# Eight start offsets, modulo 256 bytes, for the ring of split hidden features in a two-layer hybrid transformer kernel

## The chip, the cores and the metric

The kernel runs on one core of a Trainium2 chip. The metric is the device time of one execution in microseconds (us). Times of the kernel before: 1723.94 us as the median of three runs (1721.37, 1723.94 and 1724.77). TensorE (PE in the rows) multiplies, VectorE (DVE) and ScalarE (ACT) do the elementwise work, GpSimd (POOL) a little of it, and DMAs issued by SyncE (SP) bring the weights in.

## What is computed

One sequence of 256 tokens with 16 meta tokens ahead (272 in all) and 1024 features goes through two layers. Each layer is: feed-forward, mixer (a retention group and a differential attention group on one input projection), feed-forward. Then a third block follows with an attention over context and a mixture of 32 experts. The part that the change touches is the feed-forward:

```python
def swiglu(x, w_gate, w_up, w_down):
    return (jax.nn.silu(x @ w_gate) * (x @ w_up)) @ w_down

for l in range(DEPTH):                                   # DEPTH = 2, D_FF = 2816 = 22 * 128
    h = h + 0.5 * swiglu(rmsnorm(h, ffn1_norm[l]), ffn1_w_gate[l], ffn1_w_up[l], ffn1_w_down[l])
    ...                                                  # mixer
    h = h + 0.5 * swiglu(rmsnorm(h, ffn2_norm[l]), ffn2_w_gate[l], ffn2_w_up[l], ffn2_w_down[l])
```

So there are four feed-forwards, f = 0 to 3. "The middle" is silu(gate) * up, 2816 features of 272 tokens. In the last one (f = 3) the 16 meta tokens are dropped, and 256 tokens are left.

## The kernel before

**Tiles.** Features lie on the 128 partitions, tokens along the free dimension. `h` has 8 chunks of 128 features (C = 8), the middle has 22 (F = 22). Weights stream from memory through `ring`, 8 KB per partition and slot (L623 to L710 issue the loads).

**Three products for one.** Every fp32 operand a is split into a_hi, a rounded copy (ScalarE), and a_lo = a - a_hi (VectorE), both of type fp32r. The weights are split in the same way into four buffers `w_split` (L1536 on ScalarE, L2011 on VectorE). One product is then three matmuls, in `product` (L769 to L771): w_hi with x_hi, w_hi with x_lo, w_lo with x_hi. The stationary operand is 128 by 128 from `w_split`, the moving operand has 272 columns (256 where the meta tokens are left out).

**A feed-forward.** In `ffn` (L808 on) a gate and up stage of 22 steps multiplies the eight chunks `x_hi[c]`, `x_lo[c]`; then the down stage goes over the 22 chunks i of the middle. In it `part(i, o)` is one product for output chunk o, for 8 values of o, so each chunk i of the middle is the moving operand of 24 matmuls in a row, and a down stage has 22 * 8 * 3 = 528 matmuls.

**The middle's ring.** The split chunks of the middle are `hid_hi` and `hid_lo`, eight places each (`HID_SPLITS`), chunk i in place i % 8. L1602 (ScalarE, `hidden_hi`) writes the high part and L2122 (VectorE, `hidden_lo`) the low part. Place c of `hid_hi` begins at word `hid_at + c * STEP` of the tensor `arena`, where `STEP` is 320 words (1280 bytes, five times 256), and a place is 272 words long, which leaves a gap of 48 words. The helper `spaced` (L296) cuts them, and also the eight places of `x_hi` and `x_lo`.

**Start addresses.** They follow from the allocation: `ring` begins at byte 16512 of each partition and `arena` at byte 114816, both 128 modulo 256. Every weight tile in `w_split` begins at 128 modulo 256. The places of `x_hi` and `x_lo` all begin at 64 modulo 256, and those of `x_hi_late`, `x_lo_late` (the second layer's mixer) at 0; a window of 256 tokens in these begins 64 bytes later, at 64. The places of `hid_hi` and `hid_lo` all begin at 32; in f = 3, `t_at` is 8 words, so what is read begins at 64. The chunks of `y_hi`, `y_lo` are 1088 bytes apart in the first layer, so these begin at 0, 64, 128 and 192 in turn; in the second layer they are 1024 bytes apart and all begin at 64. The experts' weights that are moving operands (L1423) begin at 128 in `ring` and at 12 in `con`.

**What else hangs on the ring's end.** `hid_end` (L294) is where it stops. `mod_product` begins there (eight chunks in which ScalarE, L1615, and VectorE, L2110 and L2112, form the sums of a modulation vector, beside the gate and up stages), and `x2n` ends half there (`at_x2n = hid_end - C * SEQ`, L369): it is the normalised input of the third block, the moving operand of L1090, L1096 and L1102 and the stationary one of L1108, between about 1084 and 1213 us.

**Order.** Each engine runs its list in program order. The experts' weights (L689 to L710) are loaded from the moment that `y2_ready` has its last count, given by VectorE at L2591.

Of the kernel before, what the change touches and what calls it, by code (L numbers as in the profile page):

```python
# [15 lines left out]
META, SEQ = 16, 256  # L16
T = META + SEQ
DEPTH = 2
FF = 2816
F = FF // P  # L20
# [16 lines left out]
HALF = SLOT // 2  # L37
QUARTER = HALF // 2
HID_SPLITS = 8
STEP, LEAD, HID_LEAD = 320, 48, 8  # L40
GAP = STEP - T
ARENA = 20768
IN2_SLOTS = 11
# [189 lines left out]
def build(nc, stream_ffn, stream_in, stream_out, stream_mod, stream_in2, stream_out2, stream_expert,  # L233
# [4 lines left out]
    with ExitStack() as ctx:  # L238
# [10 lines left out]
        arena_at = nc.sbuf_base - 4 * ARENA  # L249
# [6 lines left out]
        def cut(tensor, at, *shape):  # L256

            n = int(np.prod(shape))
            piece = tensor[:, at:at + n]
            if len(shape) == 1:  # L260
                return piece
            names = "abcd"[:len(shape)]
            sizes = dict(zip(names[1:], shape[1:]))
            return piece.rearrange(f"p ({' '.join(names)}) -> p {' '.join(names)}", **sizes)
# [21 lines left out]
        def parts(name, byte, *shape):  # L286

            n = int(np.prod(shape))
            return cut(nc.alloc_sbuf_tensor_at(name, [P, n], f32r, offset=byte), 0, *shape)


        rest = C * T + LEAD + 2 * C * STEP - GAP
        hid_at = rest + F * T + HID_LEAD
        hid_end = hid_at + 2 * HID_SPLITS * STEP - GAP  # L294
        h = cut(arena, 0, C, T)
        def spaced(name, at, n):  # L296

            return [parts(f"{name}{c}", arena_at + 4 * (at + c * STEP), T) for c in range(n)]

        x_hi, x_lo = spaced("x_hi", C * T + LEAD, C), spaced("x_lo", C * T + LEAD + C * STEP, C)  # L300
        x_hi_late, x_lo_late = spaced("x_hi_late", C * T + LEAD - META, C), spaced("x_lo_late", C * T + LEAD - META + C * STEP, C)
# [6 lines left out]
        hid = cut(arena, rest, F, T)  # L308
        gate_act = cut(con, CON["axial_cos"][0], 4, T)
        warm = cut(arena, rest, 513)  # L310
        hid_hi, hid_lo = spaced("hid_hi", hid_at, HID_SPLITS), spaced("hid_lo", hid_at + HID_SPLITS * STEP, HID_SPLITS)
        assert hid_end <= ARENA and 4 * T <= CON["causal"][0] - CON["axial_cos"][0]
        ffn_sq = hid[:, F - C:]

# [256 lines left out]
        def window(f):  # L571

            return META if f == 2 * DEPTH - 1 else 0
# [177 lines left out]
        def _(pe):  # L751
# [9 lines left out]
            def norm_sum(n):  # L761

                pe.wait_ge(consts_loaded, 16)
                pe.wait_ge(sq_summed, n + 1)
                pe.matmul(ps[:, 7, 0:T], ones, (mix_sq if n % 3 == 1 else ffn_sq)[:, 0], start=True, stop=True).then_inc(sumsq_ready, 1)

            def product(to, w, k, hi, lo, first, last_):

                pe.matmul(to, w[:, 0, k], hi, start=first, stop=False)  # L769
                pe.matmul(to, w[:, 0, k], lo, start=False, stop=False)  # L770
                return pe.matmul(to, w[:, 1, k], hi, start=False, stop=last_)  # L771

            def split_half(n):

                pe.wait_ge(split_ready, n + 2)
                return w_split[n % SPLITS]

            def first_of_all(n0):

                for k in range(2):  # L780
                    w = w_split[0] if k == 0 else split_half(n0 + k)
                    for c in range(C):
                        if k == 0:
                            pe.wait_ge(x_split_ready, c + 1)
                            pe.wait_ge(split_ready, c // 4 + 1)
                        last = product(ps[:, k, 0:T], w, c, x_hi[c], x_lo[c], c == 0, c == C - 1)
                    last.then_inc(split_used, 1)

            def first_two(n, n0, banks, t=0):

                both = [split_half(n0), split_half(n0 + 1)]
                x_hi, x_lo = stream_of(n)
                for c in range(C):
                    pe.wait_ge(x_split_ready, n * C + c + 1)
                    for k in range(2):
                        last = product(ps[:, banks[k], 0:T - t], both[k], c, x_hi[c][:, 0:T - t], x_lo[c][:, 0:T - t], c == 0, c == C - 1)
                        if c == C - 1:
                            last.then_inc(split_used, 1)

            def features(n, bank, t=0):  # L800

                w = split_half(n)
                for c in range(C):
                    last = product(ps[:, bank, 0:T - t], w, c, x_hi[c][:, 0:T - t], x_lo[c][:, 0:T - t], c == 0, c == C - 1)
                last.then_inc(split_used, 1)

            def ffn(f, n):

                n0 = HALF_AT["ffn", f, 0]
                t = window(f)  # L810
                t_at = META // 2 if t else 0
                if f == 0:
                    first_of_all(n0)
                else:
                    first_two(n, n0, (0, 1), t)
                for j in range(1, F):
                    if j == 2 and f > 0:
                        norm_sum(n)
                    if j == 3:
                        pe.wait_ge(std_ready, n + 1)  # L820
                    if j >= 4:
                        pe.wait_ge(gate_up_used, f * F + j - 3)
                    if f == 2 * DEPTH - 1 and j == CTX_AT:
                        pe.wait_ge(ctx_sq_ready, 1)
                        pe.matmul(ps[:, 2 * (j % 4) + 1, 0:SEQ], ones, ctx_acc, start=True, stop=True).then_inc(ctx_summed, 1)
                    if j in PORTIONS[f]:
                        mod_portion(PORTIONS[f][j], 2 * (j % 4) + 1)
                    for k in range(2):
                        if f == 2 * DEPTH - 1 and j == CTX_AT and k == 1:
                            pe.wait_ge(ctx_std_ready, 1)  # L830
                        if f == 0 and j == 2 and k == 1:
                            norm_sum(n)
                        features(n0 + 2 * j + k, 2 * (j % 4) + k, t)
                down = n0 + 2 * F

                def part(i, o):
                    return product(ps[:, o, 0:T - t], w_split[(down + i) % SPLITS], o, hid_hi[i % HID_SPLITS][:, t_at:t_at + T - t],
                                   hid_lo[i % HID_SPLITS][:, t_at:t_at + T - t], i == 0, i == F - 1)

                for i in range(F - 2):  # L840
                    split_half(down + i)
                    pe.wait_ge(hid_split_ready, f * F + i + 1)
                    for o in (4, 5, 6, 7, 0, 1, 2, 3) if i == 0 else range(C):
                        if i == 0 and o % 2 == 0:
                            pe.wait_ge(gate_up_used, f * F + F - 3 + (o - 4) % C // 2)
                        last = part(i, o)
                    last.then_inc(split_used, 1)
                for i in (F - 2, F - 1):
                    split_half(down + i)
                    pe.wait_ge(hid_split_ready, f * F + i + 1)  # L850
                for o in range(C):
                    last = part(F - 2, o)
                    if o == C - 1:
                        last.then_inc(split_used, 1)
                    part(F - 1, o).then_inc(y_ready if o < C - 1 else split_used, 1)

            def mod_portion(p, bank, col=T):

                batch = int(p >= MOD_FIRST[1])
                n = p - MOD_FIRST[batch]  # L860
                pe.wait_ge(mod_summed, 2 * p + 2)
                if n == 0:
                    pe.wait_ge(mod_ready, batch + 1)
                for i in range(2):
                    for j in range(2):
                        own, at = 2 * n + j, 64 * i + 32 * j
                        last = pe.matmul(ps[at:at + 32, bank, col:col + P], unit_row[:, 32 - own:64 - own], mod_sums[:, p % MOD_BUFFERS, j, i * P:i * P + P],
                                         start=True, stop=True)
                last.then_inc(mod_used, 1)
# [211 lines left out]
            for l in range(DEPTH):  # L1081
                ffn(2 * l, 3 * l)
                mixer(l, 3 * l + 1)
                ffn(2 * l + 1, 3 * l + 2)
# [132 lines left out]
            for i in range(2):  # L1217
                for step in range(6):
                    for hh in range(2):
                        rows = slice(64 * hh, 64 * hh + 64)  # L1220
                        cols = slice((2 * i + hh) * 64, (2 * i + hh) * 64 + 64)
                        to, at = ps[rows, 6 + hh], i * SEQ
                        if step < 2:
                            pe.matmul(to[:, at:at + SEQ], state[rows, 2 * step + i], qx[rows, 2 * step + i], start=step == 0, stop=False)
                        elif step < 4:
                            c = step - 2
# [12 lines left out]
            for i in range(2):  # L1239
                for t in range(2):  # L1240
                    for hh in range(2):
                        head = 2 * i + hh
                        at = (2 * i + t) * P
# [56 lines left out]
            for i in range(2):  # L1300
                for j in range(4):
                    at = 8 * i + 2 * j
# [218 lines left out]
        def _(act):  # L1521
# [43 lines left out]
            def ffn(f, n):  # L1565
# [27 lines left out]
                        act.dma_start(con[:, part], tables[:, part]).then_inc(tables_loaded, 16)  # L1593

                t = window(f)
                t_at = META // 2 if t else 0

                def hidden_hi(i):
                    act.wait_ge(hid_ready, f * F + i + 1)
# [34 lines left out]
                for i in range(F - 2):  # L1634
# [8 lines left out]
                    if f == 2 * DEPTH - 1 and 0 <= i - 9 < C:  # L1643
                        c = i - 9
# [353 lines left out]
        def _(dve):  # L1998
# [74 lines left out]
            def ffn(f, n):  # L2073
# [25 lines left out]
                deviation(n)  # L2099

                t = window(f)
                t_at = META // 2 if t else 0

                def mod_add(u):

# [933 lines left out]
```

## Time and profile before

| | |
|---|---|
| median of three runs | 1723.94 us (1721.37 to 1724.77) |
| the profiled execution | 1728.39 us, of which the span of its instructions is 1726.6 us |
| granted TensorE clock, mean | 0.998 of full speed |
| TensorE matmul busy | 98% of the span, 12315 matmuls |
| VectorE busy | 57% |
| ScalarE busy | 46% |
| DMA mean rate | 247 GB/s |

The span is the time from the first to the last instruction. A matmul's row gives its start and how long it lasted; as matmuls are pipelined, these durations overlap, and what one costs is read from the distance between the starts of neighbours. Where a stretch holds nothing but such matmuls, its length over their number is that distance.

### The profile page before, as it was taken

The numbers are of one execution on the slowest core, as the hardware profiler recorded it, in microseconds if no ns is written. First come the engines' busy times: TensorE is split into PE (matmuls) and PEld (weight loads), VectorE is DVE, ScalarE is ACT, GpSimd is POOL, SyncE is SP. The second block draws the span as 40 slices with busy tenths as digits, with TensorE's granted clock in tenths as the row PEclk, the third lists the DMA queues.
The fourth block names the chain that finished last, engine by engine and source line by source line (L and its number), as shares of the span: only waits on it lengthen the run. The fifth ranks groups of instructions, "written<-read, shape, count | busy, mean of one in ns | idle before, by whom it ended". The sixth has DMA issues, their size and how long they took to land.

```text
span 1726.6 us, 30190 instructions
## 1 busy us (share of the span) xinstructions
PE 1698.7 (98%) x12315; PEld 1392.5 (81%) x12316; DVE 978.0 (57%) x1689; ACT 797.0 (46%) x1432; POOL 168.6 (10%) x173
## 2 busy tenths in 40 slices
PE   9999999999999999999999999999999999999998
PEld 8999988999999999998999999678764544445443
DVE  6776577678767777678678665476621111121111
ACT  6664455466656765665455445455621111111111
POOL 1000053210000100014413000100410000000000
PEclk9999999999999999999999999999999999999999
DMA  9555553254576577573345455032399999999997
GB/s 373 195 215 224 171 168 102 99 173 159 230 269 244 196 267 266 205 238 133 112 159 218 176 191 195 31 86 74 133 422 407 430 428 428 429 429 430 428 427 306
DMA packets 79105, 425.87 MB, mean 247 GB/s; under 512 B 16384, under 2 KB 33024, under 8 KB 42112
## 3 DMA queue, kind: packets, MB, share of 16 engines
q1 hardware_dynamic: 78400, 421.80, 63.1%
q10 hardware_dynamic: 576, 2.29, 0.3%
q8 instruction: 89, 1.46, 0.3%
q14 instruction: 40, 0.33, 0.1%
HBM read 423.02 MB, written 1.05 MB: 246 GB/s over the span
## 4 chain that ended last, share of the span: by engine, by line
PE 77%; DVE 7%; DMA 6%; ACT 5%; DVEq 3%; issue 1%; POOL 0%; POOLq 0%; SPq 0%; ACTq 0%
PE ps L769 15%; PE ps L770 14%; PE ps L771 14%; PE ps L1423 10%; DMA ring<-stream_expert 5%; PE ps L1474 5%; DVE w_split L2011 3%; PE ps L1397 3%; ACT w_split L1536 2%; PE ps L1102 2%; PE ps L1096 2%; PE ps L1108 2%; DVEq L2138 2%; PE ps L1404 1%; PE ps L1405 1%
## 5 line engine op out<-in xcount | busy, mean ns | idle before, releaser
L2011 DVE TENSOR_TENSOR w_split<-ring,w_split 128x1024 fp32r<-128x1024 f32 x335 | 420.7, 1276 | 240.3 <-ACT w_split L1536 239.7
L769 PE MATMUL ps<-x_hi,w_split 128*128 128x272 f32 (+1 forms) x1632 | 472.8, 290 | 4.6 <-DVE x_lo L2017 1.5
L770 PE MATMUL ps<-x_lo,w_split 128*128 128x272 f32 (+1 forms) x1632 | 466.5, 286 | 0.0
L771 PE MATMUL ps<-x_hi,w_split 128*128 128x272 f32 (+1 forms) x1632 | 466.3, 286 | 0.0
L1536 ACT ACTIVATE w_split<-ring 128x1024 fp32r<-128x1024 f32 x335 | 344.8, 1052 | 219.6 <-PE ps L771 218.5
L769 PEld LDWEIGHTS ps<-x_hi,w_split 128*128 128x128 f32 x1632 | 309.3, 190 | 11.3 <-issue 5.0
L770 PEld LDWEIGHTS ps<-x_lo,w_split 128*128 128x128 f32 x1632 | 308.1, 189 | 0.4 <-issue 0.2
L771 PEld LDWEIGHTS ps<-x_hi,w_split 128*128 128x128 f32 x1632 | 308.1, 189 | 0.0
L769 PE MATMUL ps<-hid_hi,w_split 128*128 128x272 f32 (+1 forms) x704 | 200.1, 284 | 0.8 <-DVE arena L2132 0.8
L771 PE MATMUL ps<-hid_hi,w_split 128*128 128x272 f32 (+1 forms) x704 | 200.0, 284 | 0.0
L770 PE MATMUL ps<-hid_lo,w_split 128*128 128x272 f32 (+1 forms) x704 | 200.0, 284 | 0.0
L1423 PE MATMUL ps<-ring,arena 128*64 128x512 f32 x704 | 187.4, 594 | 4.1 <-DMA ring<-stream_expert 3.3
L1423 PEld LDWEIGHTS ps<-ring,arena 128*64 128x64 f32 x704 | 58.7, 137 | 99.5 <-issue 93.8
L2766 DVE TENSOR_TENSOR arena<-arena,ps 128x512 f32<-128x512 f32 x16 | 11.0, 688 | 216.8 <-PE ps L1423 216.8
L769 PEld LDWEIGHTS ps<-hid_hi,w_split 128*128 128x128 f32 x704 | 132.9, 189 | 1.0 <-DVE arena L2132 1.0
L771 PEld LDWEIGHTS ps<-hid_hi,w_split 128*128 128x128 f32 x704 | 132.2, 188 | 0.0
L770 PEld LDWEIGHTS ps<-hid_lo,w_split 128*128 128x128 f32 x704 | 132.2, 188 | 0.0
L1627 ACT ACTIVATE con<-con 128x272 f32<-128x272 f32 (+1 forms) x88 | 37.7, 428 | 157.5 <-DVE con L2130 156.5
L1938 ACT ACTIVATE arena<-ps,small 128x128 f32<-128x128 f32 x64 | 24.1, 457 | 162.4 <-PE ps L1397 162.4
L1615 ACT ACTIVATE ring<-ring,small 128x256 f32<-128x256 f32 x192 | 81.3, 495 | 0.0
L1474 PE MATMUL ps<-ring,arena 128*64 128x512 f32 x352 | 78.1, 595 | 0.0
L2777 DVE SCALAR_TENSOR_TENSOR ye_lo<-ps,arena,ye_hi 128x512 fp32r<-128x512 f32 x32 | 24.0, 750 | 91.5 <-ACT ye_hi L1954 76.6
(446 smaller groups left out, 2679.6 us busy)
## 6 DMA issues: line engine op xcount, KB each, us to landing
ring<-stream_ffn SPq DMA_DIRECT2D x131, 1024.0 KB, 4.9
ring<-stream_expert SPq DMA_DIRECT2D x48, 2048.0 KB, 25.2
ring<-stream_expert SPq DMA_DIRECT2D x36, 1024.0 KB, 12.9
arena<-stream_expert SPq DMA_DIRECT2D x16, 2048.0 KB, 25.7
ring<-stream_in SPq DMA_DIRECT2D x27, 1024.0 KB, 4.8
ring<-stream_mod SPq DMA_DIRECT2D x24, 1024.0 KB, 4.9
con<-stream_expert SPq DMA_DIRECT2D x8, 2048.0 KB, 26.4
ring<-stream_out SPq DMA_DIRECT2D x12, 1024.0 KB, 4.8
```

What stands on the lines that cost most here:

```text
L769: pe.matmul(to, w[:, 0, k], hi, start=first, stop=False)
L770: pe.matmul(to, w[:, 0, k], lo, start=False, stop=False)
L771: return pe.matmul(to, w[:, 1, k], hi, start=False, stop=last_)
L1096: last = pe.matmul(ps[:, b, 0:KEYS], w[:, c], x2n[:, :, c], start=c == 0, stop=c == C - 1)
L1102: last = pe.matmul(ps[:, b, i * SEQ:i * SEQ + SEQ], w[:, i, c], x2n[:, 0, c], start=c == 0, stop=c == C - 1)
L1397: last = pe.matmul(ps[:, 6 + half, (c % 4) * P:(c % 4) * P + P], h2t[:, t, c * P:c * P + P], sel[:, t], start=t == 0, stop=t == 1)
L1423: last = pe.matmul(ps[rows, 4 + part, 0:FE], xs[:, c, rows], w, start=c == 0, stop=c == C - 1)
L1474: last = pe.matmul(ps[rows, 6 + half, 0:512], hidT[:, f, rows], w[:, half * 512:half * 512 + 512], start=f == 0, stop=f == FE // P - 1)
L1536: nc.scalar.activation(w_split[n % SPLITS][:, 0], half_of(n), ACT.Copy).then_inc(hi_ready, 1)
L1615: last = nc.scalar.activation(to[:, c], w[:, c], ACT.Identity, scale=cc[:, c, v:v + 1])
L1627: nc.scalar.activation(gate_act[:, j % 4, t:T], gate_act[:, j % 4, t:T], ACT.Silu).then_inc(gate_act_ready, 1)
L2011: nc.vector.tensor_tensor(w[:, 1], half_of(n), w[:, 0].bitcast(fp32), ALU.subtract).then_inc(split_ready, 1)
```

## The change

The common lead of 8 words (`HID_LEAD`) is dropped, and each of the eight places gets a lead of its own from `HID_PLACES`. The places then begin at 16, 48, 80, 96, 112, 144, 160 and 176 modulo 256 bytes, high and low parts alike. As a tensor is allocated at multiples of 32 bytes, `spaced` allocates at the multiple below and takes a window that starts 0 or 4 words in. `t_at` becomes 0, so f = 3 reads from the same offsets as the other three. `hid_end` grows by 40 words (160 bytes): `mod_product` and `x2n` begin at 0 modulo 256 where they began at 96. No instruction is added, removed or moved, and the operands keep their sizes.

```diff
-STEP, LEAD, HID_LEAD = 320, 48, 8
+STEP, LEAD = 320, 48
+HID_PLACES = [4, 12, 20, 24, 28, 36, 40, 44]
...
-        hid_at = rest + F * T + HID_LEAD
-        hid_end = hid_at + 2 * HID_SPLITS * STEP - GAP
+        hid_at = rest + F * T
+        hid_end = hid_at + 2 * HID_SPLITS * STEP
...
-        def spaced(name, at, n):
-
-            return [parts(f"{name}{c}", arena_at + 4 * (at + c * STEP), T) for c in range(n)]
+        def spaced(name, at, n, places=[0] * HID_SPLITS):
+
+            return [parts(f"{name}{c}", arena_at + 4 * (at + c * STEP + places[c] // 8 * 8), T + 4)[:, places[c] % 8:places[c] % 8 + T] for c in range(n)]
...
-        hid_hi, hid_lo = spaced("hid_hi", hid_at, HID_SPLITS), spaced("hid_lo", hid_at + HID_SPLITS * STEP, HID_SPLITS)
+        hid_hi, hid_lo = spaced("hid_hi", hid_at, HID_SPLITS, HID_PLACES), spaced("hid_lo", hid_at + HID_SPLITS * STEP, HID_SPLITS, HID_PLACES)
...
-                t_at = META // 2 if t else 0
+                t_at = 0
```

The last of these edits stands three times, on the TensorE, ScalarE and VectorE sides of `ffn`.

## Rows read from the trace of the kernel before

**Rows 1.** The page: span, busy time and share of each engine.
```profile
span 1726.6 us, 30190 instructions
PE 1698.7 (98%) x12315; PEld 1392.5 (81%) x12316; DVE 978.0 (57%) x1689; ACT 797.0 (46%) x1432; POOL 168.6 (10%) x173
```

**Rows 2.** Stretches of the down stages: us, busy us by engine (count), clock, DMA share, GB/s.
```profile
149.01:208.21 59.20, 59.20 (x482) 59.20 (x481) 30.47 (x38) 25.80 (x35) 0.00 (x0) 1.00 0.59 210
493.52:552.72 59.20, 59.20 (x482) 59.20 (x481) 37.96 (x47) 38.37 (x66) 0.00 (x0) 1.00 0.62 231
692.09:751.29 59.20, 59.20 (x482) 59.20 (x481) 37.89 (x46) 38.66 (x68) 0.00 (x0) 1.00 0.65 225
1022.98:1082.34 59.36, 59.36 (x506) 59.36 (x505) 36.72 (x52) 30.49 (x48) 4.58 (x5) 1.00 0.55 185
```

**Rows 3.** Who waited in the first down stage, 144 to 210 us: in total, times, longest.
```profile
ACT w_split L1536 <- PE ps L771: 32.7, 20, 1.9
DVE w_split L2011 <- ACT w_split L1536: 29.1, 21, 1.7
```

**Rows 4.** Timeline: start, us. First down stage, four neighbours (offset 32, 272 columns).
```profile
160.11 0.29 PE L770 MATMUL ps<-hid_lo,w_split 128*128 128x272 f32 x1
160.24 0.28 PE L771 MATMUL ps<-hid_hi,w_split 128*128 128x272 f32 x1
160.36 0.29 PE L769 MATMUL ps<-hid_hi,w_split 128*128 128x272 f32 x1
160.49 0.28 PE L770 MATMUL ps<-hid_lo,w_split 128*128 128x272 f32 x1
```

**Rows 5.** Timeline, offset 64, 272 columns: 313 matmuls, the first and the last.
```profile
37.59 0.29 PE L771 MATMUL ps<-x_hi,w_split 128*128 128x272 f32 x1
...
76.07 0.29 PE L771 MATMUL ps<-x_hi,w_split 128*128 128x272 f32 x1
```

**Rows 6.** Timeline, offset 0, 272 columns: 48 matmuls, the first and the last.
```profile
755.98 0.29 PE L769 MATMUL ps<-x_hi_late,w_split 128*128 128x272 f32 x1
...
761.93 0.29 PE L771 MATMUL ps<-x_hi_late,w_split 128*128 128x272 f32 x1
```

**Rows 7.** Timeline, offsets 0, 64, 128, 192 in turn: 25 matmuls, first and last.
```profile
348.06 0.29 PE L769 MATMUL ps<-y_hi,w_split 128*128 128x272 f32 x1
...
351.08 0.29 PE L769 MATMUL ps<-y_hi,w_split 128*128 128x272 f32 x1
```

**Rows 8.** Timeline, offset 64, 256 columns: 89 matmuls, the first and the last.
```profile
895.93 0.28 PE L769 MATMUL ps<-x_hi,w_split 128*128 128x256 f32 x1
...
905.91 0.28 PE L770 MATMUL ps<-x_lo,w_split 128*128 128x256 f32 x1
```

**Rows 9.** One tile and one line: duration ns min/median/max, first and last start, forms.
```profile
L2122 DVE TENSOR_TENSOR hid_lo<-arena,hid_hi x88: 411/434/1254, 38.7 to 1064.3; 128x272 fp32r<-128x272 f32 x66, 128x256 fp32r<-128x256 f32 x22
L1602 ACT ACTIVATE hid_hi<-arena x88: 400/415/418, 38.2 to 1063.1; 128x272 fp32r<-128x272 f32 x66, 128x256 fp32r<-128x256 f32 x22
```

**Rows 10.** The chain that ended last, between 49 and 70 us: start, us, what.
```profile
49.20 1.60 ACT arena L1615 x4
...
55.79 1.14 DVE arena L2110
...
61.60 1.60 ACT ring L1615 x4
...
68.19 1.14 DVE ring L2110
```

**Rows 11.** The chain, third block's projections: start, us, what.
```profile
1121.22 13.81 PE ps L1102 x64
```

**Rows 12.** Groups of the experts' stage: line, operands, count | busy us, mean ns | idle.
```profile
L1423 PE MATMUL ps<-ring,arena 128*64 128x512 f32 x704 | 187.4, 594 | 4.1 <-DMA ring<-stream_expert 3.3 <-DMA con<-stream_expert 0.8
L1423 PE MATMUL ps<-con,arena 128*64 128x512 f32 x152 | 67.3, 593 | 1.1 <-DMA arena<-stream_expert 1.1
```

**Rows 13.** DMA waits of SP: us, times, longest.
```profile
SPq L689 <- DVE arena L2591: 55.7, 1, 55.7
```

**Rows 14.** Stretch of the experts' stage, columns as in rows 2.
```profile
1265.00:1726.60 461.60, 448.45 (x2450) 213.55 (x2448) 82.56 (x207) 77.89 (x172) 1.67 (x3) 1.00 0.98 415
```

More of the change, by code:

```diff
@@ L1595, in ffn @@
                 t = window(f)
-                t_at = META // 2 if t else 0
+                t_at = 0
                 def hidden_hi(i):
@@ L2101, in ffn @@
                 t = window(f)
-                t_at = META // 2 if t else 0
+                t_at = 0
                 def mod_add(u):
```

## The prediction, made before the changed kernel was run

> **What bounds the kernel now.** I read the page first: TensorE's matmuls fill 98% of the span, 1698.7 of 1726.6 us, and VectorE and ScalarE are far below [rows 1]. The reader is to see that the order of the day is TensorE's, so a change of operand addresses counts only by what it does to the distance between two matmul starts. Next I cut the four down stages out as stretches [rows 2]. The change touches only these on TensorE. In each, TensorE is busy for the whole stretch at a granted clock of 1.00, the 2.4 GHz level, and VectorE and ScalarE for 31 to 39 of some 59 us. The waits of the first down stage say the same: ScalarE waits for TensorE to give back a weight buffer (32.7 us) and VectorE for ScalarE (29.1 us) [rows 3]. So nothing feeds TensorE late there, and a nanosecond per matmul is a nanosecond per matmul of the span.
>
> The stretches also hold the price of one matmul. Two of the 482 in the first row had started before the stretch, so 480 distances take 59.20 us: 123.33 ns, in each of the first three stages alike. In the fourth it is 504 distances in 59.36 us: 117.8 ns for 256 columns [rows 2]. At 2.4 GHz, 272 columns are 113.3 ns and 256 are 106.7 ns, so there are some 10 ns on top of each matmul. The timeline shows that these are not even: neighbours start 0.13, 0.12 and 0.13 us apart and last 0.29, 0.28 and 0.29 us [rows 4]. Something beside the columns is being waited for, and the question is whether the start address decides it.
>
> **Does an offset matter at all?** The trace of before answers in part, because operands of the same kind lie at other offsets. 272 columns at offset 64 (x): 312 distances in 38.48 us, 123.3 ns [rows 5]. At offset 0 (x_late): 47 distances in 5.95 us, 126.6 ns [rows 6]. With 0, 64, 128 and 192 in turn every three matmuls (y): 24 distances in 3.02 us, 125.8 ns [rows 7]. So offsets 32 and 64 are alike, 0 is 3.2 ns dearer, and if in y the offsets 0 and 64 cost what they cost alone (125.0 on average), 128 and 192 come to 126.7 ns on average, which contains what a change of offset costs. With 256 columns the same offset 64 is seen at two prices: 113.4 ns in the x chunks at the start of f = 3 (88 distances in 9.98 us) [rows 8], and 117.8 ns in the down stage [rows 2]. There the address is not what decides, or not alone.
>
> The Trainium skill, page "SBUF — State Buffer", section "SBUF: two separate sides", says that TensorE has its own ports and never waits on anyone. By that rule an offset has no price and the change gives the time of before. The 126.6 against 123.3 ns at the same width and clock speaks against it; no row shows which access it is that collides.
>
> **The change part by part.**
>
> *First three down stages, 3 * 528 = 1584 matmuls of 272 columns.* They go from offset 32 to eight others. None of the eight is one of 0, 32 and 64, for which I have a clean row. Bounds: from below 113.3 ns, the columns alone, which the 256-column row reaches with fewer columns; that is -10.0 ns * 1584 = -15.9 us. From above the 126.7 ns of the two unresolved offsets, +3.4 ns * 1584 = +5.4 us. The value that I take is the mean of the three clean offsets, (126.6 + 123.3 + 123.3) / 3 = 124.4 ns, since nothing says that new offsets are better or worse than those seen: +1.1 ns * 1584 = +1.7 us. The lower end is far from every row of this width, so it is not what I go by.
>
> *Fourth down stage, 528 matmuls of 256 columns.* From offset 64 at 117.8 ns to eight others. Bounds: 113.4 ns, -2.3 us, and the same 3.4 ns on top, +1.8 us. Since both prices are seen at one offset, each new place may fall into either; I take half, -2.2 ns * 528 = -1.2 us.
>
> *Changes between places.* A new place comes once in 24 matmuls, 88 times in all. In y a change comes every three matmuls, and its whole excess over 125.0 ns is 0.8 ns per matmul, 2.4 ns per change: 88 * 2.4 ns = 0.2 us at most, which I count as nothing.
>
> *Writers of the ring.* L1602 and L2122 take 415 and 434 ns in the median, over offsets 32 and 64 [rows 9]. Even doubled, 22 of each add some 9 us to engines that are idle for over 20 us of each down stage, so they cost nothing; the cover is gone only when one of them needs over 59 us in a stage.
>
> *`mod_product`, from 96 to 0.* Four products of L1615 take 1.60 us on the arena (offset 96) and 1.60 on the ring (offset 128), and L2110 takes 1.14 us on both [rows 10]. No price.
>
> *`x2n`, from 96 to 0.* It is an operand of some 400 matmuls. L1102 needs 13.81 us for 64 of 256 columns, 215.8 ns each [rows 11], twice 106.7 plus 2.4 ns: these take two cycles per column and have almost nothing on top. The experts' matmuls of the same plain kind last 594 ns with the moving operand at 128 and 593 ns at 12 [rows 12]. I take zero; as bounds, minus 0.9 us (2.4 ns on 400) and plus 4.0 us (10 ns on 400, what lies on top of a matmul in the down stage).
>
> *Behind the change.* The stage of the experts runs at a DMA share of 0.98 [rows 14], and one might think that it swallows a gain. But its loads start only when the third block's attention is done: SP waited 55.7 us for L2591 [rows 13]. Everything there shifts with TensorE, one to one.
>
> *Sum.* +1.7 - 1.2 + 0 = +0.5 us. On the profiled execution of 1728.39 us (span 1726.6 and 1.8 around it) that is 1728.9; the median of the runs shown lies 4.45 us lower, so 1724.4 us, say 1724.5.
>
> **The rivals.**
>
> *Long distances vanish (faster).* The uneven starts [rows 4] suggest two kinds of matmul, about 121 and about 126 ns. If most new offsets give only the short kind, 1584 matmuls gain 2.8 ns, 4.4 us, and if the fourth stage falls wholly to 113.4 ns, 2.3 us more: -6.7 us, 1717.2 us. For it: 113.4 ns at an offset that also gives 117.8. Against: three clean offsets of 272 columns, and none below 123.3. Chance 0.17.
>
> *Starts off a 32-byte boundary cost more (slower).* Six of the eight places (16, 48, 80, 112, 144, 176) begin at 16 modulo 32, and every fp32r operand in the trace begins at a multiple of 32. Places 0 to 5 serve three chunks of a stage and 6 and 7 two, so 17 of 22 chunks are concerned. At 3.4 ns each, the worst seen: 17/22 * 2112 * 3.4 ns = +5.5 us, 1729.5 us. It decides the result from 2.1 ns per concerned matmul. For it: no such row exists. Against: moving operands at 12 modulo 256 pay nothing, though at two cycles per column [rows 12]. Chance 0.17.
>
> *`x2n` collides (slower).* At 0, opposite the weights at 128, its 400 matmuls pay up to 10 ns: +4.0 us, 1728.5 us. Against: 2.4 ns on top at 96, and nothing between 12 and 128 [rows 11, 12]. Chance 0.04.
>
> *The offset decides nothing.* The 3.2 ns between offsets 0 and 64 come from something else in the mixer, and the phase in which TensorE enters a stretch sets the price. Then all four stages keep theirs, within 1 us: 1724 us. For it: two prices at one offset and width. Against: 123.33 ns at three stages and in x to the second digit. Chance 0.17.
>
> **How the numbers follow.** The forecast has 0.45 and the rivals 0.17, 0.17, 0.04 and 0.17. A measurement tells some 0.2% from no change, 3.4 us. The first rival is faster by more; of the forecast 0.03 lies beyond that on each side. Faster 0.17 + 0.03 = 0.20; slower 0.17 + 0.02 (half of the collision) + 0.03, about 0.21; the same 0.59. The range goes to both rivals, 1717.0 to 1729.5 us.
>
> **What would show it right or wrong.** In the trace of the changed kernel each group of 24 matmuls has its place, so every offset gives its own distance: I expect 123 to 127 ns in the first three stages, no place below 120, and a sum of each stage within 1.5 us of before. Gate and up, mixer and experts' stages keep their distances, and L1102 its 215.8 ns. Places at 16 modulo 32 dearer than 96 and 160 alone would be the second rival. I am wrong if places differ by over 8 ns, or if VectorE starts to end TensorE's waits in a down stage.

## The result and the profile after

The changed kernel takes 1729.7 us (median of five runs, 1729.35 to 1729.77), the kernel before 1723.94 us (five runs, 1721.32 to 1724.77). The ratio is 1.0032, with a 95% interval of 1.0021 to 1.0044: 5.5 us slower (the two medians are 5.8 us apart). The slowdown is clear of noise, and the time lies far above the expected 1724.5 us and right at the upper end of the range, 1729.5 us: the ratio on 1723.94 us gives 1729.5 us, and the median itself is 0.2 us beyond.

Stretches of the changed kernel, columns as in rows 2. The first four are the down stages without their first 24 and last 24 matmuls, so 480 distances each. The last three lie in the gate and up stage of f = 3 (80, 480 and 320 distances of 256 columns, all at offset 64).

```profile
148.42:208.50 60.08, 60.08 (x483) 60.08 (x481) 30.55 (x38) 25.73 (x35) 0.00 (x0) 1.00 0.59 208
494.89:554.95 60.06, 60.06 (x483) 60.06 (x482) 38.16 (x48) 38.48 (x66) 0.00 (x0) 1.00 0.63 229
695.58:755.64 60.06, 60.06 (x483) 60.06 (x481) 38.16 (x48) 38.48 (x66) 0.00 (x0) 1.00 0.66 226
1026.26:1082.89 56.63, 56.63 (x483) 56.63 (x481) 34.81 (x50) 29.13 (x45) 4.01 (x4) 1.00 0.58 191
899.44:908.86 9.42, 9.42 (x82) 9.42 (x81) 7.62 (x9) 8.18 (x15) 4.95 (x5) 1.00 0.69 255
913.77:970.31 56.54, 56.54 (x483) 56.54 (x481) 43.08 (x63) 27.04 (x40) 11.78 (x13) 1.00 0.53 189
984.87:1021.14 36.27, 36.27 (x323) 36.27 (x321) 23.08 (x33) 15.87 (x20) 0.00 (x0) 1.00 0.52 182
```

The same stretches of the kernel before, where they are not in rows 2:

```profile
1025.10:1081.63 56.53, 56.53 (x482) 56.53 (x481) 34.91 (x50) 29.15 (x45) 4.01 (x4) 1.00 0.57 192
896.73:905.79 9.06, 9.06 (x82) 9.06 (x81) 7.26 (x9) 8.13 (x15) 4.71 (x4) 1.00 0.68 247
911.07:967.60 56.53, 56.53 (x482) 56.53 (x481) 43.07 (x63) 26.82 (x39) 11.79 (x13) 1.00 0.52 188
982.23:1019.92 37.69, 37.69 (x322) 37.69 (x321) 23.14 (x33) 15.98 (x21) 0.00 (x0) 1.00 0.49 172
```

The first three down stages go from 59.20 [rows 2] to 60.06 us per 480 distances, 123.3 to 125.1 ns at the same clock. The fourth hardly moves between these two profiles, 117.8 to 118.0 ns. The gate and up stage of f = 3, which the change doesn't touch, shows two prices at one offset: 9.42 us for 80 are 117.8 ns and 36.27 us for 320 are 113.3 ns, and before and after have them in different stretches.

Cut at every place, the second down stage (chunks 8 to 15) gives the price of each offset, 24 distances to a row, in the order 16, 48, 80, 96, 112, 144, 160 and 176:

```profile
515.91:518.89 2.98, 2.98 (x26) 2.98 (x25) 1.58 (x2) 2.97 (x7) 0.00 (x0) 1.00 1.03 434
518.89:521.86 2.97, 2.97 (x26) 2.97 (x25) 1.61 (x3) 1.63 (x3) 0.00 (x0) 1.00 0.80 265
521.86:524.88 3.02, 3.02 (x26) 3.02 (x25) 2.87 (x4) 1.38 (x2) 0.00 (x0) 1.00 0.25 100
524.88:527.92 3.04, 3.04 (x26) 3.04 (x25) 2.41 (x4) 1.38 (x2) 0.00 (x0) 1.00 0.48 129
527.92:530.92 3.00, 3.00 (x26) 3.00 (x25) 1.58 (x2) 2.74 (x6) 0.00 (x0) 1.00 0.52 218
530.92:533.90 2.98, 2.98 (x27) 2.98 (x25) 1.58 (x2) 2.96 (x7) 0.00 (x0) 1.00 0.82 264
533.90:536.92 3.02, 3.02 (x27) 3.02 (x26) 1.67 (x3) 1.64 (x3) 0.00 (x0) 1.00 1.02 429
536.92:539.91 2.99, 2.99 (x26) 2.99 (x25) 2.84 (x4) 1.06 (x1) 0.00 (x0) 1.00 0.74 266
```

A place 2.96 us long would cost what it did before (24 * 123.3 ns). All eight are dearer, by 0.01 to 0.08 us. DMA share and VectorE's busy time vary from row to row and don't go with the price: 1.02 and 0.25 of DMA share stand at the same 3.02 us.

### The profile page after: what moved, and what is told of

It reads as the page before. It is cut to its first block, busy times and chain, and to the rows that moved or that the text cites. A ratio compares the mean times of both kernels' runs of the same rounds, so it can differ in the third digit from the quotient of the medians.

```text
span 1728.1 us, 30190 instructions
## 1 busy us (share of the span) xinstructions
PE 1699.1 (98%) x12315; PEld 1393.3 (81%) x12316; DVE 977.6 (57%) x1689; ACT 797.1 (46%) x1432; POOL 169.2 (10%) x173
## 4 chain that ended last, share of the span: by engine, by line
PE 82%; DMA 6%; DVE 5%; ACT 4%; issue 1%; DVEq 1%; POOL 0%; POOLq 0%; SPq 0%; ACTq 0%
PE ps L770 16%; PE ps L772 16%; PE ps L771 16%; PE ps L1424 10%; DMA ring<-stream_expert 5%; PE ps L1475 5%; PE ps L1398 3%; DVE w_split L2012 2%; PE ps L1103 2%; PE ps L1097 2%; ACT w_split L1537 2%; PE ps L1109 2%; PE ps L1405 1%; PE ps L1406 1%; DVEq L2139 1%
```

## The experiments

Each ratio is to the kernel before, run beside it, with its 95% interval in brackets. The median of the kernel before was 1723.6 us beside again, end_later, other_eight and turned_round, 1724.5 us beside first_three, last_one, all_64_later and last_at_240, 1727.7 us beside arena_64_later, one_offset_48 and steps_of_four, and 1726.9 us beside last_at_240_again. So times are compared within such a group only; the distances in ns can be compared across all traces.

**The two profiles leave a question.** The down stages explain +2.9 us (1.8 ns * 1584) and +0.1 us, and the measured step is 5.5 us. But the profiled execution of before took 1728.39 us, more than any of its timed runs then. My theory became that these runs had f = 3 at the lower of its two prices, and that the change takes this price away from the fourth down stage.

**again: the kernel before, unchanged** (no edit).

> The kernel before, unchanged. Its timed runs lie between 1721.3 and 1724.8 us, its profiled execution at 1728.39 us; the changed kernel lies at 1729.35 to 1729.77 us in all of its runs, the profiled one among them. Between the two profiles the down stages account for 1.8 ns * 1584 = +2.9 us and the fourth for 0.1 us, the gate and up stage of f = 3 gives 1.6 us back. Theory L (a lock): the matmuls of 256 columns in f = 3 run at one of two prices, 113.4 or 117.8 ns, and which one can differ from execution to execution; a profile of this kernel at 1724 us would then show some 4 us of its gate and up stage or of its fourth down stage at 113.4 ns. Theory P (the profile itself adds the 4.4 us) expects 117.8 ns there again, and the profiled time again some 4 us above the timed ones.

Measured: ratio 0.9992 (0.9976 to 1.0009). The profiled execution took 1723.75 us, with a span of 1722.1 us. Its down stages three and four and the last stretch of gate and up:

```profile
693.46:752.66 59.20, 59.20 (x482) 59.20 (x481) 38.03 (x47) 38.37 (x66) 0.00 (x0) 1.00 0.66 231
1023.10:1077.49 54.39, 54.39 (x482) 54.39 (x481) 35.30 (x50) 29.09 (x45) 3.96 (x4) 1.00 0.59 199
981.84:1018.11 36.27, 36.27 (x323) 36.27 (x321) 23.07 (x33) 15.88 (x20) 0.00 (x0) 1.00 0.53 182
```

The same program has its fourth down stage at 54.39 us for 480, 113.3 ns, where the first profile has 117.8 [rows 2]. That is 2.4 us over 528 matmuls, and the last 359 distances of gate and up give 1.6 us more, of 4.5 us between the spans. The 35 timed runs of before in this comparison fit this: 21 lie at 1721.3 to 1724.6 us, 4 between 1725 and 1727 and 10 at 1728.1 to 1731.4. Theory L holds: matmuls of 256 columns at offset 64 have two prices, and which one a stretch gets differs from execution to execution of the same program. Theory P falls; in turned_round below, the profiled execution (1727.68 us) even lies 3.2 us under the median.

This trace is also the better one to set the changed kernel against, since both have the same prices in gate and up of f = 3 (9.42, 56.54 and 36.27 us). The spans differ by 6.0 us: 2.9 us in the first three down stages and 2.5 us in the fourth (56.63 against 54.39 us for 480), and some 0.4 us in x chunks that are told of below.

**end_later: the other addresses that the change moves.**

```diff
-        hid_end = hid_at + 2 * HID_SPLITS * STEP - GAP
+        hid_end = hid_at + 2 * HID_SPLITS * STEP - GAP + 40
```

> The kernel before with hid_end alone 40 words later, so mod_product and x2n begin at 0 modulo 256 instead of 96, and the ring of the middle stays at offset 32. The theory of the collision at x2n expects up to +4 us, with distances of L1096, L1102 and L1108 above 429, 215.8 and 215.8 ns. The theory that only the ring's offsets matter expects the time of before within 0.1% and these distances unchanged, since in the profile of the changed kernel L1102 already shows its old distance.

Measured: ratio 1.0005 (0.9990 to 1.0021). The chain of this kernel shows L1102 with `x2n` at 0 modulo 256:

```profile
1121.25 13.81 PE ps L1102 x64
```

It is 13.81 us for 64, to the digit that of before [rows 11]. The collision at `x2n` is excluded, and with it and `mod_product` together the kernel stays within 0.2% of before.

**first_three and last_one: the parts of the change alone.** The ring gets one list of places for f = 0 to 2 and another for f = 3; first_three has the change's offsets in the first and 64 in the second, last_one has 32 in the first and the change's in the second.

```diff
...     # first_three, shortened
+        hid_first = spaced("hid_hi", hid_at, HID_SPLITS, HID_PLACES), spaced("hid_lo", ..., HID_PLACES)
+        hid_last = spaced("hid_hi_last", hid_at, HID_SPLITS, [16] * HID_SPLITS), spaced("hid_lo_last", ..., [16] * HID_SPLITS)
+        def hid_of(f):
+            return hid_last if f == 2 * DEPTH - 1 else hid_first
```

> The eight offsets of the change in the first three down stages alone; the fourth keeps offset 64, as before. The theory of the sum says that the change costs +2.9 us in the first three (1.8 ns * 1584) and +2.5 us in the fourth, because timed runs of before mostly have the fourth at 113.3 ns (as the profile of the unchanged kernel under the label again shows, 1722.1 us span) and the new offsets hold it at 118.0. It expects +2.9 us here, 0.17%, some 1726.5 us, with the places at 123.6 to 126.7 ns, and the fourth stage at 113.3 or 117.8. The rival, that the fourth stage has no share (117.8 against 118.0 in the first pair of profiles), expects the whole +5.5 us here.

> The reverse: the first three down stages keep offset 32 for all places, and only the fourth takes the eight offsets. The theory of the sum expects +2.5 us over the kernel before (some 1726 us), with the fourth stage at 118.0 ns in its trace whatever the state of the stages ahead of it. The rival expects no change.

Measured: first_three 1.0018 (1.0008 to 1.0027), +3.1 us; last_one 1.0015 (1.0006 to 1.0024), +2.6 us. Together 5.7 us, against 5.5 for the whole change; each of the two is known to within some 1.6 us. The third and fourth down stages of first_three, then of last_one:

```profile
696.34:756.39 60.05, 60.05 (x482) 60.05 (x481) 38.14 (x48) 38.48 (x66) 0.00 (x0) 1.00 0.65 227
1024.31:1078.71 54.40, 54.40 (x482) 54.40 (x481) 35.29 (x50) 29.11 (x45) 3.96 (x4) 1.00 0.61 199
```

```profile
695.31:754.51 59.20, 59.20 (x482) 59.20 (x481) 38.02 (x47) 38.36 (x66) 0.00 (x0) 1.00 0.67 230
1022.48:1079.11 56.63, 56.63 (x483) 56.63 (x481) 34.79 (x50) 29.13 (x45) 4.01 (x4) 1.00 0.57 191
```

Each part has its price in its own stage and nowhere else in the ring. In last_one TensorE came into the fourth stage from 113.3 ns in gate and up, and the new offsets still took it to 118.0. So the fourth stage costs up to 2.5 us (4.7 ns * 528), though the first pair of profiles shows 0.1. At offset 64 the fourth stage had the price of the last stretch of gate and up in all four traces that have it there: 117.8 ns in before and end_later, 113.3 in again and first_three. That last stretch was at 113.3 ns in eight of the eleven profiled executions with the x chunks at 64.

A small part is left over: behind the first down stage, the x chunks at offset 64 run at 126.7 ns until the next interruption, in the changed kernel and in first_three alike, while the kernel before has 123.3 ns. 96 distances of the changed kernel, then of the kernel before:

```profile
212.27:224.43 12.16, 12.16 (x98) 12.16 (x97) 10.15 (x12) 9.40 (x17) 6.42 (x6) 1.00 0.41 126
```

```profile
211.79:223.63 11.84, 11.84 (x98) 11.84 (x97) 10.06 (x12) 9.44 (x17) 6.23 (x6) 1.00 0.40 123
```

It is 0.3 us here and 0.1 us behind the second stage. The addresses are the same, so it comes from what ran before; all_64_later, with the same list of offsets, has it too, and no other trace with these chunks at 64 does. The 126.7 ns are a second price of 272 columns at offset 64, which the unchanged kernel can show as well: 44 distances between other interruptions in the trace of again:

```profile
429.63:435.21 5.58, 5.58 (x46) 5.58 (x46) 3.32 (x6) 3.93 (x7) 0.00 (x0) 1.00 0.94 393
```

**other_eight and turned_round: does the price belong to the offset?**

```diff
-HID_PLACES = [4, 12, 20, 24, 28, 36, 40, 44]
+HID_PLACES = [0, 32, 52, 56, 60, 16, 8, 48]      # other_eight
+HID_PLACES = [44, 40, 36, 28, 24, 20, 12, 4]     # turned_round
```

> The changed kernel with the other eight of the sixteen offsets: places at 0, 128, 208, 224, 240, 64, 32 and 192 modulo 256 bytes. The theory that each offset has its own price expects 126.6 ns at 0, 123.3 at 64 and 32 (as in the kernel before), about 127 at 128 and 124 to 125 at 192, and new values between 120 and 127.5 at 208, 224 and 240: a mean near 125 ns and a time of 1725 to 1730 us. A theory in which the change of offset from place to place costs the time expects 125 ns or more at 32 and 64 as well.

> The changed kernel with its list of offsets turned round, so that place 0 begins at 176 and place 7 at 16. If the price belongs to the offset, each keeps it: 124.6 ns at 16, 123.6 at 48, 125.8 at 80, 126.7 at 96, 125.0 at 112, 124.0 at 144, 125.7 at 160 and 124.8 at 176, and the three stages of 272 columns stay within 0.3 us each (places 0 to 5 serve three chunks and 6 and 7 two). If it belongs to the place in memory, or to the way from one place to the next, the prices stay with the place numbers or change all over.

Measured: other_eight 1.0025 (1.0010 to 1.0040), turned_round 1.0033 (1.0018 to 1.0047). The table holds the mean distances in ns by offset, worked out from the first starts of neighbouring places (24 distances, chunks 8 to 15 of the second and of the fourth down stage). "Turned" is the same offset in turned_round.

| offset | 272 columns | turned | 256 columns | turned |
|---|---|---|---|---|
| 16 | 124.5 | 124.5 | 118.4 | 118.9 |
| 48 | 123.7 | 126.6 | 119.5 | 119.0 |
| 80 | 125.8 | 126.7 | 119.0 | 119.2 |
| 96 | 126.7 | 126.5 | 118.4 | 118.1 |
| 112 | 125.0 | 125.0 | 117.0 | 117.3 |
| 144 | 124.0 | 124.2 | 116.8 | 116.8 |
| 160 | 125.7 | 125.8 | 116.7 | 117.1 |
| 176 | 124.8 | 125.1 | 118.1 | 118.3 |
| 0, 32, 64 (other_eight) | 126.5, 124.0, 123.4 | | 118.5, 117.2, 113.6 | |
| 128, 192, 208 (other_eight) | 125.1, 126.5, 124.8 | | 119.7, 118.0, 119.5 | |
| 224, 240 (other_eight) | 126.6, 123.7 | | 119.6, 113.3 | |

With 272 columns, six of eight offsets keep their price within 0.3 ns when the list is turned round and they lie in other places. 80 and 48 don't: turned, they follow 96 and 80, and stay near the 126.6 ns of their neighbour. So the offset decides which prices are to be had, and what ran before picks one where there are two. With 256 columns only 64 and 240 show the low price in these chunks. But 144 came near it once in each trace of the change's list: in its first turn of the fourth stage (chunk 5) it takes 114.0 ns, in its second (chunk 13) 116.8 ns. The changed kernel's 24 distances of each:

```profile
1037.64:1040.37 2.73, 2.73 (x26) 2.73 (x25) 1.47 (x3) 2.46 (x3) 0.00 (x0) 1.00 0.68 204
1060.23:1063.04 2.81, 2.81 (x27) 2.81 (x26) 1.96 (x4) 1.77 (x3) 0.00 (x0) 1.00 0.62 222
```

Not all that I expected of other_eight came: 128 was cheaper (125.1 ns, not 127), 192 dearer (126.5, not 124 to 125), and 32 cost 124.0 ns and not 123.3.

**all_64_later: the address or the distance from the weights?**

```diff
+        ahead = sb("ahead", [P, 16])
         ring = sb("ring", [P, 12 * SLOT])
```

> The changed kernel with 64 bytes allocated ahead of ring, so that weights and moving operands alike begin 64 bytes later modulo 256, and the distance between them stays. If only the distance of the two addresses counts, each place keeps its price: 124.6, 123.6, 125.8, 126.7, 125.0, 124.0, 125.7 and 124.8 ns for places 0 to 7. If the address of the moving operand alone counts, the prices go with the new offsets 80, 112, 144, 160, 176, 208, 224 and 240: 125.8, 125.0, 124.0, 125.7, 124.8, 124.8, 126.6 and 123.7 ns.

One execution, 1727.03 us. The second to fifth place (now at 112, 144, 160 and 176 modulo 256, as far from the weights as before the shift):

```profile
518.34:521.30 2.96, 2.96 (x26) 2.96 (x25) 1.61 (x3) 1.62 (x3) 0.00 (x0) 1.00 0.85 271
521.30:524.32 3.02, 3.02 (x26) 3.02 (x25) 2.87 (x4) 1.38 (x2) 0.00 (x0) 1.00 0.28 111
524.32:527.36 3.04, 3.04 (x26) 3.04 (x25) 2.41 (x4) 1.38 (x2) 0.00 (x0) 1.00 0.49 143
527.36:530.37 3.01, 3.01 (x27) 3.01 (x26) 1.58 (x2) 2.75 (x6) 0.00 (x0) 1.00 0.49 204
```

They are those of the changed kernel (2.97, 3.02, 3.04, 3.00 us). By the moving address alone they would be 3.00, 2.98, 3.02 and 3.00. From the starts, all eight places agree with the changed kernel within 0.1 ns. What counts is the distance between the start of the stationary and the start of the moving operand, modulo 256 bytes; "offset" below is the start of the moving operand with the weights at 128.

**arena_64_later: a forecast from the table.** The kernel before, with all moving operands 64 bytes further from the weights.

```diff
+        between = sb("between", [P, 16])
         arena = sb("arena", [P, ARENA])
```

> The kernel before with 64 bytes allocated between ring and arena: every moving operand begins 64 bytes later modulo 256, and the weights stay at 128. Under the label all_64_later both moved and every place kept its price to 0.1 ns, so the theory is that the distance from the weight's start to the moving operand's start sets the price. From the two surveys of sixteen offsets it expects: x of 272 columns, now at 128, 125.1 ns; the middle's ring of the first three stages, at 96, 126.6 ns; f = 3, at 128, 119.6 ns; x_late, at 64, 123.3 ns. In all 3840 * 1.8 + 1584 * 3.3 + 1554 * (119.6 - 115.5) - 408 * 3.2 ns = +17 us over the kernel before, 1.0%. A theory that the ring of the middle alone is sensitive, or that places with 16 bytes off a 32-byte boundary are, expects nothing from these shifts by multiples of 32.

Measured: ratio 1.0080 (1.0056 to 1.0103), 1740.35 us. In its trace the third down stage (offset 96), then the fourth and the gate and up stage of f = 3 (offset 128):

```profile
699.43:759.60 60.17, 60.17 (x483) 60.17 (x482) 38.12 (x47) 38.49 (x66) 0.00 (x0) 1.00 0.65 227
1034.37:1091.97 57.60, 57.60 (x483) 57.60 (x482) 34.74 (x50) 29.14 (x45) 4.05 (x4) 1.00 0.56 188
918.26:975.86 57.60, 57.60 (x482) 57.60 (x481) 43.13 (x64) 27.20 (x40) 11.79 (x13) 1.00 0.52 185
```

f = 3 at 128 is 120.0 ns (forecast 119.6), and x of 272 columns 125.3 (forecast 125.1), but for one stretch of 190 matmuls at 126.7. The ring at 96 is 125.3 ns and not the forecast 126.6: held at one offset, 96 has a second, lower price too. The total came to 0.8% where I had forecast 1.0%; in this comparison more runs of before lay at their upper prices (median 1727.66 us). The direction and most of the size follow from the table. The shift of both operands left each place's price, and the shift of one alone changed the price of every stage shown: together they are what shows that the distance of the two addresses counts.

This run also settles the rival by which the dear offset 0 was something else in the mixer: the same 47 distances of `x_hi_late` and `x_lo_late`, 5.95 us at offset 0 [rows 6], take 5.81 us at 64, 123.6 ns.

```profile
762.60:768.41 5.81, 5.81 (x50) 5.81 (x48) 5.19 (x12) 4.86 (x10) 0.02 (x1) 1.00 0.72 204
```

**one_offset_48.**

```diff
-HID_PLACES = [4, 12, 20, 24, 28, 36, 40, 44]
+HID_PLACES = [12] * 8
```

> The changed kernel with all eight places at offset 48. At 48 two prices were seen: 123.6 ns where it was entered from a place at 16, and 126.6 ns where it was entered from a place at 80. If an offset has more than one steady state and the way in picks one, each stage here holds one of the two from its first place to its last: 123.6 ns, +0.5 us, or 126.6 ns, +5.2 us over the three stages. With 256 columns 119.0 to 119.5 ns, +0.8 to +3.2 us. If the price at 48 is decided by the neighbours' addresses, it is neither.

Measured: 1.0012 (0.9998 to 1.0026), so nothing clear by time. The trace has 59.20 us for 480 in the second and the third down stage and 57.25 in the fourth. That is 123.3 ns, the price of before, and 119.3 ns.

```profile
493.42:552.62 59.20, 59.20 (x482) 59.20 (x481) 38.02 (x47) 38.35 (x66) 0.00 (x0) 1.00 0.64 231
1024.66:1081.91 57.25, 57.25 (x482) 57.25 (x481) 34.80 (x50) 29.15 (x45) 4.03 (x4) 1.00 0.56 189
```

Each stage holds one value from first place to last, as expected, and it is the lower one, 0.3 ns below that of the changed kernel. So part of what the change costs is the alternation itself: 48 held alone is as cheap as 32. Of the eight offsets two were held in a whole stage, 48 here and 96 in arena_64_later. Held, they lie 0.0 and 2.0 ns above the 123.3 ns of before, in the changed kernel 0.3 and 3.3 ns. What the other six cost when held is not known.

**steps_of_four: starts inside a line of 16 bytes.**

```diff
+HID_PLACES = [5, 6, 7, 9, 10, 11, 13, 14]      # and a window of T + 8 in spaced
```

> The changed kernel with places at 20, 24, 28, 36, 40, 44, 52 and 56 bytes modulo 256, none a multiple of 16. If the price follows lines of 16 bytes, 20, 24 and 28 cost what 16 or 32 do (124.6 or 123.3 to 124.0 ns), 36 to 44 what 32 or 48 do, and a start inside a line costs one more line at most (1 to 2 ns). If starts inside a line are dear, all eight lie above 127 ns. If it follows the address byte for byte, the prices lie between those of the neighbours, and one of them may be below 123.3 ns, which no multiple of 16 is.

One execution, 1729.43 us. By offset, 272 columns: 128.1 ns at 20, 126.8 at 24, 125.2 at 28, 126.9 at 36, 123.3 at 40 and 44, 129.3 at 52 and 127.0 at 56. The place at 40, and the dearest of all, at 52, two places behind it:

```profile
528.34:531.30 2.96, 2.96 (x27) 2.96 (x25) 1.58 (x2) 2.70 (x6) 0.00 (x0) 1.00 0.49 205
...
534.26:537.36 3.10, 3.10 (x26) 3.10 (x25) 1.75 (x3) 1.64 (x3) 0.00 (x0) 1.00 1.01 425
```

None of the three expectations fits: steps of 4 bytes can matter, by 3.6 ns between 36 and 40 (the way in may have a share in that), starts inside a line are neither all dear nor all cheap, and none is below 123.3 ns. In the 24 offsets tried, 123.3 ns is the least that 272 columns take.

**last_at_240 and last_at_240_again: f = 3 where the low price stands alone.** 32 bytes for the ring of the first three stages, 240 for the x chunks and the ring of f = 3.

```diff
...     # shortened; `hid_of` as in first_three, and gate and up of f = 3 read x_hi_last, x_lo_last
+        x_hi_last, x_lo_last = spaced("x_hi_last", C * T + LEAD - 24, C, [4] * C), spaced("x_lo_last", ..., [4] * C)
+        hid_last = spaced("hid_hi_last", hid_at, HID_SPLITS, [60] * HID_SPLITS), spaced("hid_lo_last", ..., [60] * HID_SPLITS)
```

> The kernel before with f = 3 moved to offset 240, x chunks and ring of the middle alike; the first three stages keep 32. Under the label other_eight a place at 240 with 256 columns fell to 113.3 ns although it was entered from a place at 119.6 ns, whereas at 64 both 113.3 and 117.8 are seen. If 240 has the low price alone, gate and up and down of f = 3 run at 113.3 ns in every execution: 1554 matmuls, up to 6.9 us less than the slow profile of before and some 2 to 4 us less than its median, 1720 to 1721 us, with less scatter. If both prices exist at 240 too, the time stays that of before.

> The kernel with f = 3 at offset 240 once more, on a chip and at a time of its own. If 240 has the low price alone, its runs lie between 1720.5 and 1723 us again, while the kernel before, beside it, scatters over 1721.5 to 1729 us, and the trace shows 113.3 to 113.8 ns in gate and up and down of f = 3 again. If the first profile was a lucky execution, some runs lie at 1725 to 1729 us.

Measured: 1722.05 us, ratio 0.9988 (0.9979 to 0.9997), and 1722.16 us, ratio 0.9976 (0.9965 to 0.9988). Eleven runs lie at 1720.6 to 1722.7 us and ten at 1721.6 to 1724.1, spreads of 2.1 and 2.5 us, where the runs of before beside them spread over 3.8 and 7.7 us. The first time is above the 1720 to 1721 us that I expected. The stretches of f = 3 in the second trace, 80, 480, 320 and 480 distances:

```profile
896.78:905.84 9.06, 9.06 (x82) 9.06 (x81) 7.26 (x9) 8.13 (x15) 4.73 (x4) 1.00 0.64 238
911.10:965.50 54.40, 54.40 (x482) 54.40 (x481) 42.95 (x63) 26.77 (x39) 11.86 (x13) 1.00 0.57 197
979.78:1016.04 36.26, 36.26 (x322) 36.26 (x321) 23.09 (x33) 15.90 (x20) 0.00 (x0) 1.00 0.52 181
1021.03:1075.43 54.40, 54.40 (x483) 54.40 (x481) 35.33 (x50) 29.12 (x45) 3.98 (x4) 1.00 0.61 199
```

All are at 113.3 ns. This version lies 0.1 to 0.2% below before. It was not run beside the change; by the two ratios to before it would be some 0.4% below that.

## Why the prediction was right, and where it was not

**The number.** The measured time reaches the upper end of the range, and it does so by luck: that end came from the rival of the 32-byte boundary, which the traces exclude. The forecast itself was +0.5 us, with "the same" at 0.59, and the result is +5.5 us, more than the 0.2% that I had named as what can be told from no change; "slower" had 0.21 (its terms add up to 0.22). The mechanism, a price of the offset in the down stages, was right. The sum built on it was not, by the terms below.

**TensorE bounds the down stages.** Right. Its stretches stay full, and VectorE ends no wait of TensorE there but one of 0.8 us at the start of the first stage, which before has too. A reading was off: VectorE and ScalarE are busy for 26 to 39 us of a stretch [rows 2], not 31 to 39, which changes nothing.

**The offset has a price.** Right: there are 118 to 120 ns and 113.3 ns at one width and clock, and all_64_later and arena_64_later show that the price goes by the distance of TensorE's own two operands. The Trainium skill, page "SBUF — State Buffer", section "SBUF: two separate sides", says that TensorE never waits on anyone. I took that to mean that an offset has no price, and this case's traces don't bear that reading out. They don't show TensorE waiting for another engine either, and no run shows an access that collides.

**First three down stages.** The direction was right and the term was undersized: +1.1 ns expected, +1.8 measured, +2.9 instead of +1.7 us. The mean of three clean offsets was the failed step. Two of these three, 32 and 64, cost the least of the 24 offsets tried (123.3 ns), so the kernel before stood at the floor of this price, and a sample with two floors in it underrates any other mix. The bounds held: all eight places lie between 123.6 and 126.7 ns.

**Fourth down stage.** Here a step failed in sign. I took -1.2 us, half-way to the low price, because the profile had 117.8 ns. At offset 64 the stage has 113.3 ns in two of four traces, and at the new offsets 118.0 in all three that have the change's list: up to +2.5 us, and +2.6 us by last_one. That most timed runs of before had 113.3 ns is inferred from their times and from last_one; no trace of them exists. The two prices at one offset were in my rows [rows 2, 8], and I asked which one the change would reach and not which one the timed runs had. I also expected gate and up to keep their distances, and in f = 3 they differ from execution to execution.

**Profile against median.** I subtracted 4.45 us as if it were the cost of profiling. Profiling has no such cost: the changed kernel, again and the two traces at 240 have their profiled time within 2 us of the group in which most of their timed runs lie, and turned_round's lies below its median. What the traces show in its place is the upper price in f = 3, 4.0 us between the profiles of before and of again. The sum of terms was thus set against an execution that was not the typical one.

**Places, writers, `mod_product`, `x2n`.** I had changes of place at nothing, 0.2 us at most, and this term failed too: at 48 and 96, 0.3 and 1.3 ns per matmul come with the alternation. If these two stood for all eight, which no run shows, that would be 0.8 ns * 1584 = 1.3 us, an estimate, of the 2.9 us in the first three stages. The x chunks behind a stage add some 0.4 us, also at nothing in my sum. `x2n` and `mod_product` cost nothing that end_later can show, and the writers end no wait of TensorE.

**The rivals.** "Long distances vanish" fell: nothing is below 123.3 ns in 24 offsets. "Starts off a 32-byte boundary" fell as a mechanism, though it gave almost the right time, 1729.5 us: 48 and 144, both off, are the cheapest of the change, and 96, on it, is the dearest. The collision at `x2n` fell by end_later. "The offset decides nothing" fell by first_three, last_one and arena_64_later, but its idea, that the way in sets the price, holds where an offset has two.

## What to carry to other kernels

Before a term is set against a median, see whether the profiled execution belongs to the group in which most timed runs lie; of the 4.45 us between the two here, the two prices in f = 3 explain 4.0 us. Where every fp32r matmul brings a new stationary operand, as here, the distance of the two operands' starts modulo 256 bytes is worth trying: it moves a matmul by up to some 5%, to be read from the distances of starts in one trace with several offsets. A trace that changes the offset every 24 matmuls gives a first survey only; hold the chosen offset for a whole stage before trusting its price. Prefer an offset that has shown only one price over one that is sometimes as good.

## What the runs showed of the hardware that I had not expected

- With fp32r operands and 128 stationary columns, 272 moving columns take 123.3 to 129.3 ns and 256 take 113.3 to 120.4 ns at a granted clock of 1.00 (the 2.4 GHz level), by the distance of the two start addresses modulo 256 bytes and by what ran before. Shifting both by 64 bytes changes no place by over 0.1 ns. That shift is the only one of both that was tried, and the period of 256 is an assumption that fits: places 1280 bytes apart, five times 256, have one price where all have one offset (one_offset_48).
- The price has memory: with 272 columns offset 48 gives 126.6 ns behind a dear place, 123.7 behind a cheaper one and 123.3 when held, offset 96 gives 126.7 in the alternation and 125.3 when held, and offset 64 with 256 columns gives 113.3 or 117.8 ns from one execution of the same program to the next. What picks it in a given execution stays open; within the x chunks it was seen to change at interruptions only, as between the 9.42 and the 36.27 us stretches above.
- The plain fp32 matmuls of 256 columns, at 215.8 ns, took no notice of a shift from 96 to 0.
